# Dense tokens first through the mixer, dense key rankings beside the gathered tokens' mixer, u tiles and rows spread anew, and another order of the gate matrix

## The chip, the cores and the metric

The kernel runs on one core of a Trainium2 chip. The metric is the device time of one execution in microseconds. Times of a kernel are given as the median of several runs; the profile is of one more execution.

## The reference, cut to what matters

One layer of a hybrid decoder over 512 prompt tokens and 64 sample tokens (8 sequences of 8). The mixer is a sliding-window attention with sinks beside a convolution module; after it comes PEER, a retrieval of single-neuron experts.

```python
def layer(x):
    xn = rms_norm(x, norm1_g)
    q, k, v, glu = _project(xn, w_in, q_norm_g, k_norm_g)
    a = attention(q, k, v, sinks)                     # window 128; samples also see 128 cached keys
    c = _conv_module(pad(glu), w, b, ln_g, ln_b, pw)  # depthwise, width 31, then layer norm, silu, @ pw
    h = x + concat(rms_norm(a), rms_norm(c)) @ w_out
    return h + _peer(rms_norm(h, norm2_g), wq, keys, u, v)

def _peer(xt, wq, keys, u, v):                        # u, v: 16384 experts x 1024
    q = (xt @ wq).reshape(T, 8, 2, 128)
    s = einsum('thpd,hpnd->thpn', q, keys)            # 8 heads x 2 halves x 128 keys
    ts, ti = top_k(s, 16)
    best_s, pos = top_k(all 256 sums of the two halves' scores, 16)
    idx, gate = the experts of pos, softmax(best_s)
    hu = einsum('chkd,cd->chk', u[idx], xt)
    return einsum('chk,chkd->cd', gelu(hu) * gate, v[idx])
```

## The kernel before

The 576 tokens stand in five tiles of `TILES`. Tiles 0 to 2 (tokens 0 to 383, `DT` = 384) are the dense tokens: for them u and v are multiplied whole, 128 tiles of 128 experts each, and a gate matrix picks the experts. Tiles 3 and 4 (`TA`, `TB`, 128 + 64 tokens, `GT` = 192) are the gathered tokens: GpSimd fetches, for each of 384 rows, the u or v vectors of 128 token-expert pairs with an indirect DMA into a ring of `SLOTS` = 8, and VectorE multiplies and sums them (`row`).

All order is written out by hand, each engine running its own list, tied by semaphores. The stages, with their starts in the profile:

- The mixer for all 576 tokens. Its matmuls take the columns in two halves of 288 (`HALF`, `two`). After the projections come eight attention units `u` (block of 128 queries, key-value head): scores `S` (L590), softmax on VectorE (`softmax_max`, `softmax_div`) with the exponentials on ScalarE, transposes `PT` (L601), values `O` (L612). Between these TensorE computes the GLU's gemms or the taps of the last conv channel block, and VectorE the taps of the other three (`conv_quarter`, L1457), in slots given by `CONV_AT`. Then the sample attention `SS`, `PTS`, `OS`, and the tail: means, variances, pointwise and output gemms (L524), the second norm (L1224).
- The gathered tokens' queries and key scores (`wqa`, `sca`, 16 blocks) with the rankings `key_ranks("a", ..)`: five VectorE instructions for each tile and block (L1245 to L1249). From 410 us.
- `picks(TA)` and `picks(TB)`: the best 16 of the sums, and the experts' numbers. Between their parts stand calls of `low(n)` (L1234), the low half of u tile `n`, which TensorE's `dense_u(n)` waits for (24 matmuls, L711). 17 u tiles (`U_TOP`), and the first two dense query blocks. From about 485 us.
- 16 blocks of dense queries, scores and rankings (`wqb`, `scb`, `key_ranks("b", ..)`, three tiles), each with one u tile and three rows (`ROWS_RANK`). From about 583 us.
- `picks` of the three dense tiles, 12 u tiles and 6 rows each. From about 731 us.
- The gate stage: 64 batches (`NBAT`) of 6 tokens: VectorE writes two tables of ones (`onehots`, L1397), ScalarE puts the gates in (L997), TensorE multiplies them (L761), ScalarE copies the product to `Gs` (L1013), and SP stores four batches at a time. 54 u tiles (`u_at`) and 152 rows (`batch_rows`) are spread over the batches. From about 891 us.
- The v stage: for each of 128 tiles `mt` = gelu x gates (L1420), its high and low parts `ah` (ScalarE) and `al` (L1428), `low` of the v tile (L1234), 18 matmuls (L783), and the rest of the rows (`v_rows`, 166). The gates come in groups of 16 expert rows (`JG`), two groups in `Gl`; the 16 loads of a group are issued one per tile during the group before (`load_gates`). From about 1284 us.

PSUM is handed out by `psum_plan` as four pairs of banks; `take`, `ready`, `R` and `F` tie each use to the one before it. SP's list holds the weight loads (`load_block`, ring of four), the u and v tiles (`load_raw`, three), and the stores.

Of the kernel before, what the change touches and what calls it, by code (L numbers as in the profile page):

```python
# [43 lines left out]
SLOTS = 8  # L44
# [16 lines left out]
U_RANK = U_TOP + NM  # L61
U_GATE = U_RANK + 12 * DTI
# [8 lines left out]
ROWS_RANK = 3  # L71
ROWS_PICK = 6
B_ROW0 = ROWS_RANK * NM + ROWS_PICK * DTI
V_ROW0 = B_ROW0 + 152

# [13 lines left out]
EXP_AFTER = {6: TA, 14: TB, 39: 0, 51: 1, 63: 2}  # L89
KEYS_AFTER = {8: TB, 33: 0, 45: 1, 57: 2}  # L90
GELU_AFTER = {29: 0, 56: 1}
# [20 lines left out]
BLOCKS += ["woa0", "woa1", "woa2", "pw0", "pw1"] + [f"woa{_m}" for _m in range(3, DC)] + [f"wob{_m}" for _m in range(DC)]  # L112
NMIX = len(BLOCKS)
ROW_WO = BLOCKS.index("woa0") + 2
BLOCKS += [f"wqa{_m}" for _m in range(NM)] + [f"wqb{_m}" for _m in range(NM)]


def block_row(n):

    name = BLOCKS[n]  # L120
    if name[:2] == "wo":
        return ROW_WO + int(name[3:])
    if name[:2] == "pw":
        return ROW_WO - 2 + int(name[2:])
    return n if n < NMIX else ROW_WO + DC + (n - NMIX) % NM


def block_use(n):
# [6 lines left out]
    return {"pw0": "pw1", "pw1": "pw3"}.get(name, name)  # L135


CONV_AT = [0, 0, 0, 1, 2, 3, 4, 5, 6, 7, 8, 9, 10, 11, 12, 12, 12]
# [6 lines left out]
def psum_plan():  # L145

    plan = [("ms1", 3), ("K", 0), ("Q0", 1), ("Kn", 3), ("Q1", 2), ("Q0n", 3), ("Q2", 0), ("Q1n", 3), ("Q3", 1),
            ("Q2n", 3), ("V", 2), ("Q3n", 3)]
    for u in range(8):
        plan += [(f"S{u}", 2)] + ([(f"glu{2 * u}", 0)] if u < CC else []) + [(f"PT{u}", 3)]  # L150
        plan += ([(f"glu{2 * u + 1}", 1)] if u < CC else []) + [(f"O{u}", 2)]
    plan += [("taps", 0)]
    plan += [("SS", 2), ("PTS", 3), ("OS", 2), ("msA", 3), ("mean", 0), ("woa0", 2), ("var", 1)]
    plan += [("woa1", 3), ("woa2", 2), ("pw0", 0), ("pw1", 1), ("pw2", 3), ("pw3", 0), ("woa3", 2), ("msC", 1)]
    plan += [("woa4", 3), ("woa5", 0), ("woa6", 2), ("woa7", 3)]
    plan += [(f"wob{m}", m % 3) for m in range(DC)]
    plan += [("ms2", 3)]
    for m in range(NM):
        plan += [(f"wqa{m}", m % 2)]
        if m:  # L160
            plan += [(f"sca{m - 1}", 2 + (m - 1) % 2)]
# [8 lines left out]
def hymba_peer(nc, xT_d, wblk_d, cols_d, maskp_d, masks_d, ident_d, ckT_d, cv_d, state_d, keysT_d, u_d, v_d, uT_d,  # L170
# [7 lines left out]
    with ExitStack() as ctx:  # L178
# [188 lines left out]
        def _(sp):  # L367
# [72 lines left out]
            for m in range(NM):  # L440
                if m < RAWS:
                    load_raw(m)
# [1090 lines left out]
```

## Time and profile before

| | |
|---|---|
| median of 3 runs | 1841.26 us (1835.47 to 1842.4) |
| the profiled execution | 1849.16 us, span 1847.3 us |
| TensorE busy | 1669.8 us, 90% |
| VectorE busy | 1432.0 us, 78% |
| ScalarE busy | 770.1 us, 42% |
| GpSimd busy | 550.0 us, 30% |
| DMA | 477.45 MB, mean 258 GB/s |
| granted TensorE clock, mean | 0.953 |

The span is from the first to the last instruction of the profiled execution. Busy time is the time in which an engine has at least one instruction under way; matmuls are pipelined, so the distance between the starts of two of them is shorter than their durations, and the same holds, less so, for VectorE. `PE` is TensorE's matmuls, `PEld` its weight loads, `DVE` VectorE, `ACT` ScalarE, `POOL` GpSimd, `SP` the engine that issues most DMAs.

### The profile page before, as it was taken

Reading aid. Unit: us, or ns where it says so; the run is one execution under the profiler, and the core shown is the slowest. Engines: PE = TensorE matmul, PEld = TensorE weight load, DVE = VectorE, ACT = ScalarE, POOL = GpSimd, SP = SyncE. Lnnn points to the kernel's source line nnn. Section 1 sums busy time; section 2 is a strip of 40 time slices with the busy share of each in tenths; the row PEclk is TensorE's granted clock in tenths of the full one; section 3 lists DMA queues with packets and bytes.
Section 4 is the critical chain, followed back from the end, with each engine's and each line's share of the span. In section 5 each row is a group of like instructions: output and inputs, shape, how many; then the busy total and the mean of one; then the engine's idle time right before and its main releaser. Section 6 shows DMA issues by size and latency. Waiting matters only on the chain.

```text
span 1847.3 us, 23140 instructions
## 1 busy us (share of the span) xinstructions
PE 1669.8 (90%) x8361; PEld 1447.9 (78%) x8361; DVE 1432.0 (78%) x2657; ACT 770.1 (42%) x1274; POOL 550.0 (30%) x395
## 2 busy tenths in 40 slices
PE   7887678989699998999889898998999999999997
PEld 5766446769697877999889898998877877877876
DVE  3466854338778999787899999994888888988976
ACT  3222112212242222444789888883333333333332
POOL 0000000000011333111477676661344443443430
PEclk9998887999899999999999999999999999999999
DMA  6110500125275877777699999999999999999985
GB/s 192 46 46 1 66 1 13 50 68 194 89 247 184 277 281 228 248 235 234 216 415 407 406 413 402 381 403 389 363 371 371 375 362 381 387 358 365 379 306 184
DMA packets 164360, 477.45 MB, mean 258 GB/s; under 512 B 28063, under 2 KB 61535, under 8 KB 162071
## 3 DMA queue, kind: packets, MB, share of 16 engines
q1 hardware_dynamic: 108951, 274.63, 42.7%
q0 software_dynamic: 55296, 201.35, 28.7%
q8 instruction: 67, 1.10, 0.2%
q14 instruction: 46, 0.38, 0.1%
HBM read 420.93 MB, written 54.42 MB: 257 GB/s over the span
## 4 chain that ended last, share of the span: by engine, by line
PE 55%; DVE 33%; issue 5%; ACT 3%; DMA 2%; SPq 0%; DVEq 0%; ACTq 0%
PE ps L783 24%; PE ps L711 14%; PE ps L524 9%; DVE ring L1349 8%; DVE lo L1234 4%; DVE acc L1353 2%; DVE gA L1397 2%; DVE gB L1397 2%; DVE cacc L1457 2%; DVE tsi L1246 2%; PE ps L536 2%; DVE tsi L1249 2%; DVE sm L1247 2%; DVE tsv L1248 1%; DMA gelu_matrix<-gest 1%
## 5 line engine op out<-in xcount | busy, mean ns | idle before, releaser
L1057 POOL DMA_INDIRECT ring<-in_u,idx x192 | 281.6, 1467 | 889.1 <-DVE ijg L1329 528.4
L1234 DVE TENSOR_TENSOR lo<-raw,hi 128x1024 fp32r<-128x1024 f32 x256 | 312.9, 1222 | 138.3 <-ACT hi L916 132.2
L916 ACT ACTIVATE hi<-raw 128x1024 fp32r<-128x1024 f32 x256 | 270.4, 1056 | 330.7 <-PE ps L783 323.9
L711 PE MATMUL ps<-xh,hi 128*128 128x384 f32 x1024 | 356.1, 348 | 28.2 <-DVE lo L1234 20.2
L1057 POOL DMA_INDIRECT ring<-in_v,idx x192 | 266.9, 1390 | 369.4 <-DVE acc L1353 351.2
L711 PE MATMUL ps<-xl,hi 128*128 128x384 f32 x1024 | 348.0, 340 | 0.0
L711 PE MATMUL ps<-xh,lo 128*128 128x384 f32 x1024 | 347.5, 339 | 0.0
L783 PE MATMUL ps<-hi,ah 128*128 128x512 f32 x768 | 241.6, 396 | 23.1 <-DVE al L1428 23.0
L1353 DVE SCALAR_TENSOR_TENSOR acc<-ring,hu,acc 128x1024 f32<-128x1024 f32 x192 | 245.6, 1279 | 1.6
L783 PE MATMUL ps<-lo,ah 128*128 128x512 f32 x768 | 240.0, 394 | 0.0
L783 PE MATMUL ps<-hi,al 128*128 128x512 f32 x768 | 239.6, 394 | 0.0
L1349 DVE CUSTOM_DVE_ANT_0 ring<-ring,xtok 128x1024 f32<-128x1024 f32 x192 | 226.2, 1216 | 0.3 <-DVE hu L1349 0.3
L711 PEld LDWEIGHTS ps<-xh,hi 128*128 128x128 f32 x1024 | 197.7, 193 | 31.0 <-DVE lo L1234 22.9
L711 PEld LDWEIGHTS ps<-xl,hi 128*128 128x128 f32 x1024 | 197.2, 193 | 0.0
L711 PEld LDWEIGHTS ps<-xh,lo 128*128 128x128 f32 x1024 | 196.6, 192 | 0.0
L783 PEld LDWEIGHTS ps<-hi,ah 128*128 128x128 f32 x768 | 146.2, 191 | 56.6 <-DVE lo L1234 20.9
L783 PEld LDWEIGHTS ps<-lo,ah 128*128 128x128 f32 x768 | 146.6, 191 | 31.1
L783 PEld LDWEIGHTS ps<-hi,al 128*128 128x128 f32 x768 | 146.3, 190 | 31.0
L942 ACT ACTIVATE gest<-ps 128x384 f32<-128x384 f32 x128 | 63.4, 495 | 251.8 <-PE ps L711 210.7
L681 PE MATMUL ps<-xn,wring 128*128 128x192 f32 (+1 forms) x512 | 133.6, 416 | 5.6 <-DVE xn L1224 5.6
L1013 ACT ACTIVATE Gs<-ps 128x768 f32<-128x768 f32 x64 | 132.3, 2067 | 0.5 <-PE ps L761 0.5
L761 PE MATMUL ps<-gB,gA 128*128 128x128 f32 x768 | 103.3, 288 | 32.0 <-issue 18.4
(176 smaller groups left out, 1971.8 us busy)
## 6 DMA issues: line engine op xcount, KB each, us to landing
raw<-in_uT SPq DMA_DIRECT2D x128, 512.0 KB
raw<-in_v SPq DMA_DIRECT2D x128, 512.0 KB
wring<-in_wblk SPq DMA_DIRECT2D x48, 512.0 KB
gelu_matrix<-gest SPq DMA_DIRECT2D x64, 384.0 KB
gate_matrix<-Gs SPq DMA_DIRECT2D x16, 1536.0 KB
Gl<-gate_matrix SPq DMA_DIRECT2D x128, 192.0 KB
gel<-gelu_matrix SPq DMA_DIRECT2D x128, 192.0 KB
wring<-in_wblk SPq DMA_DIRECT2D x16, 256.0 KB
```

Source lines behind the costliest of these rows:

```text
L524: mm = nc.tensor.matmul(out[:, a * 512:a * 512 + HALF], w, rhs[:, k, a * HALF:(a + 1) * HALF], start=(k == 0), stop=(k == kc - 1))
L681: mm = nc.tensor.matmul(out[:, 0:w], wring[:, n % RING, k * P:(k + 1) * P], xn[:, k, t0:t0 + w], start=(k == 0), stop=(k == DC - 1))
L711: mm = nc.tensor.matmul(out, a[:, n % 2, w], b[:, c, :], start=(c == 0 and k == 0), stop=(c == DC - 1 and k == 2))
L761: mm = nc.tensor.matmul(ps[b % ABUF][:, c:c + NKEY], A[:, b % ABUF, t, :], B[:, b % ABUF, t, :], start=True, stop=True)
L783: mm = nc.tensor.matmul(ps[t][:, h * 512:(h + 1) * 512], a[:, n % 2, w], b[:, n % 2, h * 512:(h + 1) * 512], start=False, stop=(n == NKEY ...
L916: nc.scalar.activation(hi[:, s % 2, :], raw[:, s % RAWS, :], ACT.Copy).then_inc(s_hi, 1)
L1013: nc.scalar.activation(dst, src, ACT.Copy).then_inc(s_gev, 1)
L1057: pool.indirect_dma_start(ring[:, r % SLOTS, :], None, table, bass.IndirectOffsetOnAxis(idx[:, t, c:c + 1], 0)).then_inc(g_in[r % SLOTS], 16)
L1234: nc.vector.tensor_tensor(lo[:, s % 2, :], raw[:, s % RAWS, :], hi[:, s % 2, :].bitcast(F32), ALU.subtract).then_inc(s_lo, 1)
L1349: nc.vector.tensor_tensor_reduce(got, got, xtok[:, t, :], 1.0, 0.0, ALU.mult, ALU.add, hu[:, t, c:c + 1]).then_inc(g_used, 1)
L1353: nc.vector.scalar_tensor_tensor(out=acc[:, t, :], in0=got, scalar=hu[:, t, c:c + 1], in1=acc[:, t, :], op0=ALU.mult, op1=ALU.add).then_in ...
L1397: nc.vector.tensor_tensor(dst[:, b % ABUF], iota.unsqueeze(1).broadcast_to([P, BATCH, NKEY]), kT3[:, half, tok:tok + BATCH].unsqueeze(2).b ...
```

## The change

- The dense tokens pass the mixer first: attention units 0 to 5, the conv module and the output gemms for tokens 0 to 383 (`conv_a`, `group_gemm`, 384 columns). The units 6 and 7, the sample attention and the mixer of the 192 gathered tokens (`conv_b`, `mgb`, `ATb`, `caccb`) come after, with the 16 blocks of dense queries, scores and rankings between their parts on every engine (`block_b`, `ranks_b`).
- Then the gathered tokens' queries and rankings, as before. The two stages between the picks of the gathered and the dense tokens go: the picks of the dense tokens take 15 u tiles and 15 rows each. 61 u tiles and 130 rows are left for the gate stage, and 209 rows for the v stage.
- PSUM is planned by single banks (`held`, `after`, `region`).
- `Gs` and `Gl` hold, within a group of 16 expert rows, the token outside and the expert row inside. ScalarE's copy of a batch now writes runs of 16 elements, where it wrote single elements 24 apart; `mt` reads one element in 16 of `Gl`, where it read runs of 24. The transfers keep their sizes and runs.
- The ring has 7 slots; the gelu over the rows of the second gathered tile moves into the v stage. SP's list follows, with the first three u tiles fetched ahead of weight block `wo4`.

The diff, cut to its core:

```diff
-SLOTS = 8
+SLOTS = 7
-U_RANK = U_TOP + NM
-U_GATE = U_RANK + 12 * DTI
+U_PICK = 15
+U_GATE = U_TOP + U_PICK * DTI
-ROWS_RANK = 3
-ROWS_PICK = 6
-B_ROW0 = ROWS_RANK * NM + ROWS_PICK * DTI
-V_ROW0 = B_ROW0 + 152
+ROWS_PICK = 15
+B_ROW0 = ROWS_PICK * DTI
+V_ROW0 = B_ROW0 + 130
-GELU_AFTER = {29: 0, 56: 1}
+GELU_AFTER = {44: 0}
+GELU_IN_V = {13: 1}
-CONV_AT = [0, 0, 0, 1, 2, 3, 4, 5, 6, 7, 8, 9, 10, 11, 12, 12, 12]
+CONV_AT = [0, 0, 0, 2, 4, 6, 8, 10, 12, 12, 12, 12, 12]
...
-            Gs = gb("Gs", [P, 2, NKEY, TBLK])
-        Gl = sb("Gl", [P, 2, NBLK, JG, TBLK])
+            Gs = gb("Gs", [P, 2, NG, TBLK, JG])
+        Gl = sb("Gl", [P, 2, NBLK, TBLK, JG])
...
@@ sync: load_gates, and the loads ahead of the picks
+                             gm_d[b].rearrange("p j t -> p (j t)")[:, g * JG * TBLK:(g + 1) * JG * TBLK]).then_inc(
+                if BLOCKS[n] == "wo4":
+                    sp.wait_ge(s_o2, 16 * 15)
+                    for r in range(RAWS):
+                        load_raw(r)
...
@@ tensor: after units 0 to 5 and the dense tokens' mixer
+            def block_b(m):
+                queries(f"wqb{m}", 0, DT)
+                if m:
+                    scores("b", m - 1, range(DTI))
+            block_b(0)
+            block_b(1)
+            unit_transposes(6)
+            unit_scores(7)
+            block_b(2)
+            unit_values(6)
+            block_b(3)
+            unit_transposes(7)
+            sample_scores()
+            block_b(4)
+            unit_values(7)
+            pe.wait_ge(s_conv_b, CC)
+            group_means("meanb", lambda k: caccb[:, k, :], CC)
+            block_b(5)
+            sample_transposes()
+            block_b(6)
+            group_means("varb", conv_b, CC, s_sqc, base=CC)
+            sample_values()
+            block_b(7)
+            group_means("msAb", lambda k: mgb[:, k, :], CC, s_sqa, base=CC)
+            for m in range(CC):
+                group_gemm(f"pwb{m}", lambda k: caccb[:, k, :], CC, cut=(m % 2) * CC, last=(m % 2 == 1), made=s_sw, base=CC)
+            block_b(8)
+            group_means("msCb", conv_b, CC, s_sqcr, base=CC)
+            block_b(9)
+            for m in range(DC):
+                group_gemm(f"wo{m}", lambda k: mgb[:, k, :], DC, made=None if m else s_mg, base=DC)
+                if m >= 2:
+                    square_mean("ms2b", m - 2, DC, DT, GT)
+                if m == 3:
+                    block_b(10)
+            square_mean("ms2b", DC - 2, DC, DT, GT)
+            block_b(11)
+            square_mean("ms2b", DC - 1, DC, DT, GT)
+            for m in range(12, NM):
+                block_b(m)
...
-            for m in range(NM):
-                if m + 2 < NM:
-                    queries(f"wqb{m + 2}", 0, DT)
-                if m + 1 < NM:
-                    scores("b", m + 1, range(DTI))
-                dense_u(U_TOP + m)
-            for n in range(U_RANK, U_GATE):
+            for n in range(U_TOP, U_GATE):
                 dense_u(n)
...
@@ scalar: the copy of a gate batch
-                dst = Gs[:, i % 2, :, o:o + BATCH].rearrange("p j (a t) -> p a t j", a=2)
-                src = ps[b % ABUF][:, :].rearrange("p (a c) -> p a c", a=2)[:, :, 0:3 * NKEY].rearrange(
-                    "p a (t j) -> p a t j", t=3)
+                dst = Gs[:, i % 2, :, o:o + BATCH, :].rearrange("p g t j -> p t g j")
+                src = ps[b % ABUF][:, 0:BATCH * NKEY].rearrange("p (t g j) -> p t g j", t=BATCH, g=NG)
...
@@ vector: the order after the dense tokens' second norm
+            unit_max(6)
+            conv_b(22)
+            conv_b(23)
+            unit_div(6)
+            for c in range(DC):
+                x_low(c)
+            ranks_b(0)
+            unit_max(7)
+            ranks_b(1)
+            unit_div(7)
+            unit_out(6)
+            ranks_b(2)
...
+            unit_out(7)
+            centred("meanb", lambda c: caccb[:, c, :], CC)
+            ranks_b(3, 4, 5)
+            rstd("varb", rsb[:, 1, :])
+            normed(lambda c: caccb[:, c, :], rsb[:, 1, :], CC)
...
+            ranks_b(6)
+            rstd("msAb", rsb[:, 0, :])
+            merged(lambda c: mgb[:, c, :], lambda c: ATb[:, c, :], "ga", rsb[:, 0, :])
+            ranks_b(7)
+            rstd("msCb", rsb[:, 1, :])
...
+            ranks_b(8)
+            for m in range(4):
+                h_added("wo", m, DC, DT, GT)
+            ranks_b(9)
+            for m in range(4, DC):
+                h_added("wo", m, DC, DT, GT)
+            ranks_b(10)
+            rstd("ms2b", rsb[:, 0, :])
+            for c in range(DC):
+                second_norm(c, DT, GT, rsb[:, 0, :])
+            ranks_b(*range(11, NM))
...
-            for m in range(NM):
-                key_ranks("b", m, range(DTI))
-                low(U_TOP + m + 1)
-                for r in range(ROWS_RANK * m, ROWS_RANK * (m + 1)):
-                    row(r)
             for t in range(DTI):
-                r0 = ROWS_RANK * NM + ROWS_PICK * t
-                picks(t, t, range(U_RANK + 12 * t + 1, U_RANK + 12 * t + 13), range(r0, r0 + ROWS_PICK))
+                u0 = U_TOP + U_PICK * t + 1
+                picks(t, range(u0, u0 + U_PICK), range(ROWS_PICK * t, ROWS_PICK * (t + 1)))
...
-                                        Gl[:, g % 2, :, n % JG, :], ALU.mult).then_inc(s_mu, 1)
+                                        Gl[:, g % 2, :, :, n % JG], ALU.mult).then_inc(s_mu, 1)
```

## Rows read from the trace of the kernel before

**Rows 1.** Busy time by stage; stage, length, busy of PE, PEld, DVE, ACT, POOL, clock, DMA, GB/s.
```profile
86.00:274.00 188.00, 142.62 (x604) 102.98 (x602) 127.74 (x270) 36.71 (x92) 0.00 (x0) 0.90 0.17 28
...
274.00:297.00 23.00, 14.82 (x136) 12.00 (x136) 4.30 (x11) 3.14 (x11) 0.00 (x0) 0.61 0.00 1
297.00:410.00 113.00, 104.16 (x417) 80.45 (x417) 40.17 (x40) 25.20 (x35) 0.00 (x0) 0.97 0.17 54
410.00:485.00 75.00, 64.78 (x356) 58.44 (x357) 63.70 (x273) 15.98 (x58) 0.00 (x0) 0.89 0.46 148
485.00:583.00 98.00, 88.79 (x461) 81.70 (x460) 68.34 (x232) 42.79 (x50) 10.59 (x10) 0.95 0.52 168
583.00:731.00 148.00, 141.77 (x667) 113.56 (x666) 138.64 (x456) 36.10 (x59) 50.92 (x44) 1.00 0.78 272
731.00:891.00 160.00, 155.18 (x884) 153.75 (x885) 124.50 (x341) 72.47 (x88) 26.59 (x21) 0.98 0.75 236
891.00:1248.00 357.00, 323.68 (x2045) 321.02 (x2044) 347.63 (x460) 310.48 (x556) 242.09 (x150) 0.96 0.98 386
...
1284.00:1847.00 563.00, 534.40 (x2304) 438.77 (x2303) 471.22 (x550) 188.88 (x256) 213.65 (x157) 0.97 0.94 350
```
**Rows 2.** Timeline of TensorE: start us, duration us, engine, line, operation, count; second part near 419 us.
```profile
641.39 0.34 PE L711 MATMUL ps<-xl,hi 128*128 128x384 f32 x1
...
645.38 5.32 PE L681 MATMUL ps<-xn,wring 128*128 128x384 f32 x16
650.54 0.83 PE L691 MATMUL ps<-keysT,q2T 128*128 128x128 f32 x6
651.12 0.42 PE L711 MATMUL ps<-xh,hi 128*128 128x384 f32 x1
...
418.95 2.87 PE L681 MATMUL ps<-xn,wring 128*128 128x192 f32 x16
```
**Rows 3.** Timeline of VectorE, one block's two rankings; then the taps in the groups by line.
```profile
452.89 0.29 DVE L1245 MAX8 tsv<-sm 128x8 f32<-128x128 f32 x1
...
456.64 0.30 DVE L1245 MAX8 tsv<-sm 128x8 f32<-128x128 f32 x1
...
L1457 DVE SCALAR_TENSOR_TENSOR cacc<-gpad,cols_sb,cacc 128x512 f32<-128x512 f32 x90 | 67.6, 751 | 2.9
L1457 DVE SCALAR_TENSOR_TENSOR cacc<-spad,cols_sb,cacc 128x64 f32<-128x64 f32 x90 | 25.1, 279 | 0.0
```
**Rows 4.** Timeline of VectorE in the gate stage: a row, then two one-hot tables.
```profile
1002.11 1.21 DVE L1349 CUSTOM_DVE_ANT_0 ring<-ring,xtok 128x1024 f32<-128x1024 f32 x1
...
1003.26 0.94 DVE L1397 TENSOR_TENSOR gA<-cols_sb,kT 128x768 f32<-128x768 f32 x1
1004.13 0.94 DVE L1397 TENSOR_TENSOR gB<-cols_sb,kT 128x768 f32<-128x768 f32 x1
```
**Rows 5.** Timeline of VectorE at a group change of the v stage; then TensorE's waits there.
```profile
1350.01 0.56 DVE L1420 TENSOR_TENSOR mt<-gel,Gl 128x384 f32<-128x384 f32 x1 [3.45 <-issue]
1350.48 1.28 DVE L1353 SCALAR_TENSOR_TENSOR acc<-ring,hu,acc 128x1024 f32<-128x1024 f32 x1
1351.68 1.22 DVE L1234 TENSOR_TENSOR lo<-raw,hi 128x1024 fp32r<-128x1024 f32 x1
1352.82 0.55 DVE L1428 TENSOR_TENSOR al<-mt,ah 128x384 fp32r<-128x384 f32 x1
...
PE ps L783 <- DVE al L1428: 23.0, 8, 4.9
```
**Rows 6.** GB/s in 40 equal slices: the v stage, then the gate stage.
```profile
GB/s 304 358 391 391 341 364 400 400 398 309 378 335 404 399 309 371 396 399 388 362 356 402 397 389 320 376 369 400 396 292 375 353 400 400 267 286 342 274 76 149
...
GB/s 36 185 271 413 419 423 409 413 411 417 425 405 407 384 404 384 408 413 420 412 422 410 411 408 413 397 407 385 403 417 379 385 385 342 409 419 414 406 366 406
```
**Rows 7.** ScalarE's groups by line and shape in the gate stage: busy us, mean ns.
```profile
L1013 ACT ACTIVATE Gs<-ps 128x768 f32<-128x768 f32 x63 | 130.2, 2067 | 0.5 <-PE ps L761 0.5
...
L916 ACT ACTIVATE hi<-raw 128x1024 fp32r<-128x1024 f32 x52 | 54.6, 1051 | 3.3 <-DMA raw<-in_uT 3.3
```

More of the change, by code:

```diff
@@ L145, in psum_plan @@
 def psum_plan():
[L147 to L153, printed above, removed]
@@ L537, in means, with group_means @@
                                               src(k)[:, a * HALF:(a + 1) * HALF], start=(k == 0), stop=(k == n - 1))
+                mm.then_inc(ready, 1)
+            def group_means(name, src, n, made=None, base=0):
+                out, ready = take(name)
+                for k in range(n):
+                    if made is not None:
+                        pe.wait_ge(made, base + k + 1)
+                    rhs = src(k)
+                    mm = nc.tensor.matmul(out[:, 0:rhs.shape[1]], on512[:, :], rhs, start=(k == 0), stop=(k == n - 1))
                 mm.then_inc(ready, 1)
@@ new lines, in _, with square_mean @@
+            group_gemm("woa0", attn_a, CC, made=s_mg)
+            group_means("msC", conv_a, CC, s_sqcr)
+            for m in range(1, DC):
+                group_gemm(f"woa{m}", attn_a, CC)
+            group_gemm("wob0", conv_a, CC, made=s_mg, base=CC)
+            group_gemm("wob1", conv_a, CC)
+            def square_mean(name, m, base, t0, w):
+                if m == 0:
+                    take(name)
+                out, ready = region(name), R[use[name][0]]
+                pe.wait_ge(s_sqh, base + m + 1)
+                mm = nc.tensor.matmul(out[:, 0:w], on1024[:, :], xn[:, m, t0:t0 + w], start=(m == 0), stop=(m == DC - 1))
+                if m == DC - 1:
+                    mm.then_inc(ready, 1)
@@ L713, in dense_u, with sample_scores @@
                 mm.then_inc(s_hud, 1)
+            def sample_scores():
+                out, ready = take("SS")
+                for b in range(NDB):
+                    for g in range(NKV):
+                        grp, slot = b // 2, (b % 2) * 2 + g
+                        rows = slice(g * HD, (g + 1) * HD)
+                        o = out[slot * 32:slot * 32 + 32, (grp // 2) * 512 + (grp % 2) * 192:]
+                        q = qS[rows, b * 32:(b + 1) * 32]
+                        nc.tensor.matmul(o[:, 0:WIN], q, ckT[rows, b, :], start=True, stop=True)
+                        mm = nc.tensor.matmul(o[:, WIN:WIN + NS], q, kT[rows, SEQ:T], start=True, stop=True)
+                mm.then_inc(ready, 1)
@@ new lines, in merged @@
+            def merged(dst, src, gain, r):
+                for c in range(CC):
+                    nc.vector.scalar_tensor_tensor(out=dst(c), in0=src(c), scalar=col(gain, c), in1=r,
+                                                   op0=ALU.mult, op1=ALU.mult).then_inc(s_mg, 1)
+            def attn_added(m):
+                p = ready(f"woa{m}")
+                nc.vector.tensor_tensor(hT[:, m, 0:DT], hT[:, m, 0:DT], p[:, 0:DT],
+                                        ALU.add).then_inc(F[use[f"woa{m}"][0]], 1)
@@ L1250, in key_ranks, with picks @@
                 dve.sem_inc(s_l1, 1)
-            def picks(t, slot, lows, rows=()):
+            def picks(t, lows, rows=()):
                 n = RANKED.index(t)
@@ L1258, in picks @@
                 rows = list(rows)
+                share = len(lows), len(rows)
                 def pause():
```

850 lines of the change are left out of this document (490 added, 360 removed).

## The prediction

> **What bounds the kernel now.** I read the busy time by stage first [rows 1]; its columns show which engine fills each stretch. Up to 485 us no engine is full. In the attention units (86 to 274 us) TensorE works 142.6 of 188 us and VectorE 127.7: they take turns. In the mixer's tail (297 to 410) TensorE works 104 of 113 us while VectorE works 40. In the ranking of the gathered tokens' keys (410 to 485) VectorE works 63.7 and TensorE 64.8 of 75 us. From 583 to 891 TensorE is the bound (142 of 148 us, 155 of 160). In the gate stage (891 to 1248) it is VectorE: 348 of 357 us, with TensorE at 324. In the dense v stage (1284 on) it is TensorE again, and there VectorE is 84% busy. Then I read the rate of each kind of step from the timelines [rows 2 to 5], and last the traffic: the DMA queues move about 400 GB/s in most slices of the v stage, at most 404, and 405 to 425 in the gate stage [rows 6]. I read both as lids, close to what the stages ask for.
>
> **The profiled run and the median.** The sum is made against the profiled execution: span 1847.3 us, 1849.2 with what lies around it. The median of the shown runs is 1841.3, so what I get is multiplied by 0.9957.
>
> **Units of cost.** One u tile is 24 matmuls; 23 steps from 641.39 to 645.38 us give 4.17 us. A dense query block takes 5.16 us and its scores 0.58; a block for the 192 gathered tokens 2.87 [rows 2]. Ranking one block's keys takes VectorE 3.75 us for the two gathered tiles [rows 3], so some 5.6 for the three dense ones. A tap of the convolution costs 0.75 + 0.28 us less overlap, 0.98, for 512 and 64 columns [rows 3]; by the slope between the two shapes the 384 columns now done alone cost 0.65 and the gathered 128 + 64 cost 0.58. A u-kind row is 1.15 us and a one-hot table 0.87 [rows 4]; in the v stage mt is 0.47, a v row 1.20, low 1.14, al about 0.47 [rows 5].
>
> **Units and the dense tokens' mixer.** Columns are split 384 + 192 instead of 288 + 288, so TensorE's work is the same. The units 1 to 3 now take 16 taps of 0.65 us (10.4) in each slot where 8 of 0.98 stood (7.8). These lie on the path, since TensorE waits there for the probabilities; I take 9 us more, and unit 4 starts at 192 instead of 183. Only two more units follow, with all the taps: 46 instead of 91 us. The sample attention (23 us [rows 1]) and the units 6 and 7 move behind. The tail needs two thirds of its 104 us, 70, plus a chain of roots, reciprocals and norms of about 13: 83 us. The dense query blocks start at 321 us, where the first query block of before starts at 410.
>
> **Gathered mixer beside the dense key rankings.** TensorE gets 16 x 5.74 = 92 us of query blocks and about 60 of mixer: a third of the tail (35), two units (11), sample attention (14). VectorE gets 16 x 5.6 = 90 us of rankings and about 45 of softmax, norms and additions. Each queue is in order and each block's ranking needs the block before it, so the two don't add up to a perfect overlap: walking both queues, VectorE waits some 6 us each at rankings 6, 7, 9 and 10, and finishes ranking 10 and the second norm at 463 us. SP's weight loads follow in the same order, four deep, one per 5.7 us, and the first three u tiles are fetched behind block wo3, long before they are used. After 463 VectorE alone is late: 5 x 5.6 + 16 x 3.75 + two lows = 90 us. The picks of the gathered tokens begin at 553, against 485 before.
>
> **Picks.** The stretch 485 to 583 loses two query blocks and one score block (10.9 us): 87. The stretch 583 to 731 goes: its 16 query blocks are done, and its 16 u tiles are spread. The dense picks take 45 u tiles instead of 36, and 45 rows instead of 18: 45 x 4.17 = 188 us of TensorE and, at the 160 of before for 36, a little over, 200. VectorE has 160 there. The gate stage begins at 553 + 87 + 200 = 840 us instead of 891: 51 us gained, of which 29 are seven tiles moved on.
>
> **Gate stage.** VectorE: 64 x 1.74 + 61 lows x 1.14 + 130 rows x 1.15 = 331 us (before, with 54 lows, 126 such rows and 26 v rows, 349 of 357). TensorE: 61 x 4.17 = 254 plus the gate matmuls, 324 - 54 x 4.17 = 99 at most, less where fewer idle spells lower the clock: 341 to 353. ScalarE's Gs copy is 2.07 us for 768 elements written one by one at a distance of 96 bytes, while 1024 elements in a row take 1.05 [rows 7]; in runs of 64 bytes I expect 0.9 to 1.2, and even at 2.07 it stays just under TensorE. I take 351; the stage ends at 1191, the unchanged tail behind it (36 us) at 1227.
>
> **v stage: where part of it is given back.** 209 rows instead of 166 fall here, 43 more. VectorE: 128 x 2.08 + 17 x 1.15 + 192 x 1.20 = 516 us, before 465, and about 3 us at each of seven group changes, where mt waits for the gates' transfer: 23 us of TensorE's idle time stand there [rows 5]. The first to the last v matmul takes 553 us. The traffic: 128 x (512 + 192 + 192 KB) + 209 x 512 KB = 227 MB, less 9 MB fetched before the stage; at 403 GB/s 541 us, before 485. VectorE 537, TensorE 553 and the queues 541 now lie within 3%. The gate stage, in that position, ran 2.4% over its fullest engine. I take 569 plus 10 for the end: 579 instead of 563.
>
> **Edits at nothing.** The ring of gathered rows has seven slots instead of eight. In the v stage a row is due every 2.7 us, so seven slots still give 19 us from issue to use; if a gather took longer, each row would wait for it. The gelu over the second tile's rows moves from the gate stage into tile 13 of the v stage, on ScalarE, which is busy 189 of 563 us there [rows 1], well ahead of its first use at row 320. The copy of the gathered queries (qB) stands behind the last norm, while TensorE waits for nothing of it until unit 6.
>
> **mt's strided read.** mt now reads Gl one element every 64 bytes. No row of before shows such a read on VectorE. From below its cost is nothing: runs of 24 elements cost as much as a plain tile, 0.55 us in both L1420 and L1428 [rows 5]; a gain has no source. From above it is the price of the strided write on ScalarE, 2.69 ns an element all in, 1.03 us for 384, so 0.48 more, 61 us for 128 [rows 7]. I take nothing, since the read is on VectorE itself and the run-broken read next to it costs nothing, and keep the other end.
>
> The write row is [rows 7]. The Trainium skill, page SBUF — State Buffer, section Door 1: The DMA port swizzle, says that each access that crosses to a new 16-byte line pays a penalty; this speaks against the change. The trace agrees for ScalarE's write, 2.07 us; for VectorE's read no run here shows it. By that rule the sum would be the second case below; without it, the first.
>
> **The sum and the rivals.**
> First case, 50%: 553 + 87 + 200 + 351 + 36 + 579 = 1806 us of span, 1808 with what lies around, times 0.9957: 1800. Its own range is 1782 to 1820.
> Second, the strided read costs as the strided write does, 27%: VectorE becomes the bound of the v stage, 516 + 61 + 21 = 598, with waits 604, plus 10: span 1841 at this end, 1829 at a price of 0.38 us an instruction. Time 1823. For it: the factor of the write; against it: another engine and direction.
> Third, the other side, 7%: the read costs over 0.6 us more in each mt. From mt = 1.13 us on the v stage eats the whole gain: 1227 + 516 + 31 + 128 x 0.58 = 1848. At 1.5 us the time is 1227 + 547 + 122 = 1896 of span, 1890. Against it: it is over the highest price per element in the trace.
> Fourth, the v stage takes the extra rows in VectorE's spare time and the queues give more than 403 GB/s, 10%: v stage 563, gate stage 347, span 1786: 1780. The gate stage's 425 GB/s speaks for it, the flat slices against it.
> Fifth, the gathered mixer and the rankings don't interleave, 6%: if each in-order queue stands still while the other does its mixer part, half of the 60 us of mixer comes on top: 1806 + 27, time 1827. For it: TensorE and VectorE take turns so in 86 to 274 us.
>
> **Numbers.** The likeliest is 1800. The range 1772 to 1834 holds the first, the fourth, the fifth and most of the second; the third is left out. About 0.5% (9 us) is what a measurement can tell from no change: faster means under 1832. First and fourth wholly, three quarters of the second and half of the fifth: 0.83. Within 0.5%: 0.09. Slower: 0.08.
>
> **What would show it.** The dense query blocks should start at 321 and the picks of the gathered tokens at 553 us; VectorE should have no wait over 7 us between. The gate stage should be 345 to 355 us long and bound by TensorE; Gs near 1 us. mt decides between the first three cases: 0.55, about 1.0, or over 1.13 us. In the v stage look for rows that wait for their gathers and for GB/s over 403. The forecast is wrong if the picks start after 575, or if the v stage exceeds 600.

## The result, and the profile after

| | before | after |
|---|---|---|
| median | 1845.51 us (20 runs) | 1856.54 us (20 runs) |
| ratio | | 1.0046, 95% interval 1.0026 to 1.0066 |
| profiled span | 1847.3 us | 1862.6 us |
| TensorE, VectorE, ScalarE, GpSimd busy | 1670, 1432, 770, 550 us | 1685, 1488, 707, 705 us |
| granted TensorE clock, mean | 0.953 | 0.951 |

The forecast was 1800 us in a range of 1772 to 1834. The changed kernel is slower than the kernel before by about half a per cent, so sign and range are both wrong. Everything up to the v stage came as forecast; the v stage took 638 us instead of 569, in the profiled execution. That execution took 1864.5 us, 8 over the median (three slow ones of the 20, the longest 3344.5 us, are left out of the ratio), so the stage is up to that much shorter in others.

Busy time by stage of the kernel after, which answers to [rows 1]: stage, length, busy of PE, PEld, DVE, ACT, POOL, clock, DMA, GB/s.

```profile
86.00:191.00 105.00, 82.84 (x339) 63.38 (x340) 76.11 (x137) 22.19 (x51) 0.00 (x0) 0.91 0.07 21
191.00:320.00 129.00, 116.27 (x420) 69.41 (x418) 87.02 (x234) 28.16 (x57) 0.00 (x0) 0.96 0.34 71
320.00:460.00 140.00, 136.59 (x686) 101.38 (x687) 95.33 (x355) 41.62 (x100) 0.00 (x0) 0.95 0.30 98
460.00:552.00 92.00, 81.32 (x427) 69.57 (x426) 81.36 (x384) 16.28 (x57) 0.00 (x0) 0.95 0.31 98
552.00:637.00 85.00, 73.91 (x410) 72.86 (x408) 60.89 (x209) 42.48 (x48) 7.30 (x7) 0.93 0.53 172
637.00:833.00 196.00, 189.34 (x1081) 187.10 (x1081) 161.41 (x387) 86.69 (x110) 58.14 (x45) 0.99 0.88 291
834.00:1180.00 346.00, 341.60 (x2203) 340.99 (x2203) 327.11 (x444) 239.39 (x561) 196.25 (x128) 0.98 0.99 382
1181.00:1214.00 33.00, 30.38 (x192) 30.09 (x192) 10.38 (x13) 9.72 (x14) 3.86 (x3) 1.00 1.03 399
1214.00:1852.00 638.00, 562.86 (x2304) 449.22 (x2303) 549.71 (x607) 190.76 (x254) 437.38 (x201) 0.93 0.93 343
```

The gate stage is 5 us shorter than before (346.9 against 352.2, from its first to its last matmul) and starts 62 us earlier. In the last row no engine is full: TensorE works 563 of 638 us, VectorE 550, and the queues move 343 GB/s, less than before [rows 1]. The granted clock is 0.93 there and was 0.97 before; in e10 below, where the waits of mt and of the rows are gone, it is 0.99. GpSimd works 437 us for 201 gathers, where it worked 214 for 157. So I looked for who waits for whom there. The waits of the kernel after in the v stage (us in total, times, longest us):

```profile
POOL ring L1249 <- DVE acc L1613: 134.0, 96, 9.1
PEld ps L913 <- DVE lo L1466: 88.1, 33, 8.2
PE ps L913 <- DVE al L1738: 77.7, 34, 7.8
ACT hi L1030 <- DMA raw<-in_v: 53.3, 16, 4.7
DVE acc L1613 <- DMA ring<-in_v,idx: 34.0, 7, 7.4
DVE mt L1730 <- issue: 32.7, 7, 7.7
```

TensorE's wait for `al` was 23.0 us in 8 pieces before [rows 5]; now it is 77.7 in 34. Three things delay VectorE itself: the group changes (mt, 7 times), late v tiles (through `hi`), and rows that wait for their gathers. The last two are new: in the v stage of the kernel before, neither `hi` nor a row stands among the waits for a transfer. The timelines of GpSimd and VectorE at one such wait:

```profile
1388.61 2.15 POOL L1249 DMA_INDIRECT ring<-in_v,idx  x1 [0.64 <-DVE acc L1613]
1391.41 17.92 POOL L1249 DMA_INDIRECT ring<-in_v,idx  x1 [0.65 <-DVE acc L1613]
1409.64 0.94 POOL L1249 DMA_INDIRECT ring<-in_v,idx  x1 [0.31 <-issue]
...
1406.46 1.27 DVE L1613 SCALAR_TENSOR_TENSOR acc<-ring,hu,acc 128x1024 f32<-128x1024 f32 x1
1407.66 0.84 DVE L1730 TENSOR_TENSOR mt<-gel,Gl 128x384 f32<-128x384 f32 x1
1414.83 1.28 DVE L1613 SCALAR_TENSOR_TENSOR acc<-ring,hu,acc 128x1024 f32<-128x1024 f32 x1 [6.33 <-DMA ring<-in_v,idx]
```

One instruction that writes out a gather lasts 17.92 us, where the ones next to it last 0.94 to 2.15. VectorE works without a gap meanwhile (five tiles), uses up the ring, and then stands still for 6.3 us. 21 of the 201 gathers last over 3 us, 169 us together; before, the longest lasted 2.75 us.

The two shapes that the new order of the gate matrix changes, in the groups by line and shape of the kernel after: VectorE in the v stage, then ScalarE in the gate stage, which answers to [rows 7].

```profile
L1730 DVE TENSOR_TENSOR mt<-gel,Gl 128x384 f32<-128x384 f32 x127 | 105.5, 830 | 32.7 <-issue 32.7
L1738 DVE TENSOR_TENSOR al<-mt,ah 128x384 fp32r<-128x384 f32 x127 | 70.4, 554 | 0.0
...
L1203 ACT ACTIVATE Gs<-ps 128x768 f32<-128x768 f32 x63 | 50.0, 794 | 1.8 <-PE ps L891 1.8
```

The strided read takes 0.83 us, 0.28 more than `al` of the same size. The copy in runs of 64 bytes takes 0.79 instead of 2.07 us.

### The profile page after: what moved, and what is told of

It reads as the page before. It is cut to its first block, busy times and chain, and to the rows that moved or that the text cites. A ratio compares the mean times of both kernels' runs of the same rounds, so it can differ in the third digit from the quotient of the medians.

```text
span 1862.6 us, 23354 instructions
## 1 busy us (share of the span) xinstructions
PE 1685.0 (90%) x8361; PEld 1439.8 (77%) x8361; DVE 1487.5 (80%) x2788; ACT 707.1 (38%) x1310; POOL 705.2 (38%) x395
## 4 chain that ended last, share of the span: by engine, by line
PE 53%; DVE 22%; DMA 11%; issue 7%; ACT 4%; POOL 3%; DVEq 0%; SPq 0%; ACTq 0%
PE ps L763 24%; DMA ring<-in_v,idx 7%; PE ps L913 6%; PE ps L543 5%; PE ps L891 4%; DVE acc L1613 4%; PE ps L559 4%; POOL ring L1249 3%; PE ps L733 3%; DMA raw<-in_v 2%; DVE lo L1466 2%; DVE al L1738 2%; DVE cacc L1321 2%; ACT hi L1030 1%; PE ps L624 1%
## 5 line engine op out<-in xcount | busy, mean ns | idle before, releaser
L1249 POOL DMA_INDIRECT ring<-in_v,idx x192 | 424.9, 2213 | 167.9 <-DVE acc L1613 134.0
L913 PE MATMUL ps<-hi,ah 128*128 128x512 f32 x768 | 253.3, 412 | 77.8 <-DVE al L1738 77.7
L913 PE MATMUL ps<-lo,ah 128*128 128x512 f32 x768 | 247.8, 405 | 0.0
L913 PE MATMUL ps<-hi,al 128*128 128x512 f32 x768 | 245.1, 401 | 0.0
L913 PEld LDWEIGHTS ps<-lo,ah 128*128 128x128 f32 x768 | 151.2, 197 | 33.7
L913 PEld LDWEIGHTS ps<-hi,al 128*128 128x128 f32 x768 | 150.5, 196 | 33.5
L733 PE MATMUL ps<-xn,wring 128*128 128x384 f32 (+1 forms) x512 | 136.3, 421 | 6.2 <-DVE xn L1455 4.1
L1730 DVE TENSOR_TENSOR mt<-gel,Gl 128x384 f32<-128x384 f32 x128 | 106.3, 830 | 33.1 <-issue 32.7
L733 PEld LDWEIGHTS ps<-xn,wring 128*128 128x128 f32 x512 | 91.1, 194 | 43.3 <-issue 11.2
```

The costliest lines, as they stand in the source:

```text
L733: mm = nc.tensor.matmul(out[:, 0:w], wring[:, n % RING, k * P:(k + 1) * P], xn[:, k, t0:t0 + w], start=(k == 0), stop=(k == DC - 1))
L913: mm = nc.tensor.matmul(ps[t][:, h * 512:(h + 1) * 512], a[:, n % 2, w], b[:, n % 2, h * 512:(h + 1) * 512], start=False, stop=(n == NKEY ...
L1249: pool.indirect_dma_start(ring[:, r % SLOTS, :], None, table, bass.IndirectOffsetOnAxis(idx[:, t, c:c + 1], 0)).then_inc(g_in[r % SLOTS], 16)
L1730: nc.vector.tensor_tensor(mt[:, n % 2, :].rearrange("p (a b) -> p a b", a=NBLK), gel[:, n % EG, :].rearrange("p (a b) -> p a b", a=NBLK), ...
```

## The experiments

Each time is a median, each ratio is to the kernel before on the same chip. The two lengths are from the first to the last matmul of the stage in the profiled run. That is one execution: most are within 2 us of their median, but those of after, before, e3 and e9 are 8, 4, 2 and 4 us over it, and those of e2, e6 and e8 5, 11 and 4 under. "Gathers" is how many of GpSimd's gather instructions in the v stage last over 3 us, and the longest.

| kernel | us | ratio (95%) | gate | v | gathers |
|---|---|---|---|---|---|
| before | 1845.5 | | 352.2 | 552.6 | 0, 2.8 |
| after | 1856.5 | 1.0046 (1.0026 to 1.0066) | 346.9 | 637.8 | 21, 17.9 |
| e1_old_layout | 1842.9 | 0.998 (0.9955 to 1.0004) | 360.5 | 601.9 | 0, 2.8 |
| e2_before_new_layout | 1852.3 | 1.0034 (1.0005 to 1.0063) | 347.5 | 553.7 | 11, 7.6 |
| e3_before_7_slots | 1843.2 | 0.9998 (0.9982 to 1.0013) | 350.1 | 552.4 | 0, 2.7 |
| e4_before_209_rows | 1885.7 | 1.02 (1.0149 to 1.0252) | 341.7 | 603.8 | 0, 3.0 |
| e5_after_166_rows | 1831.3 | 0.9917 (0.9888 to 0.9946) | 388.0 | 557.9 | 7, 4.1 |
| e6_half_v_tiles | 1834.7 | 0.9957 (0.9929 to 0.9985) | 346.8 | 596.8 | 33, 17.9 |
| e7_short_low | 1822.5 | 0.9889 (0.9872 to 0.9905) | 344.1 | 599.0 | 3, 4.6 |
| e8_old_layout_166_rows | 1813.4 | 0.9865 (0.9819 to 0.991) | 381.3 | 544.7 | 0, 2.8 |
| e9_after_early_gates | 1831.8 | 0.9941 (0.9913 to 0.997) | 347.0 | 608.7 | 24, 17.9 |
| e10_old_layout_early_gates | 1803.7 | 0.9773 (0.9725 to 0.982) | 358.6 | 564.5 | 0, 2.8 |
| e11_old_166_early_gates | 1793.5 | 0.9715 (0.9669 to 0.9762) | 385.6 | 524.7 | 0, 2.8 |
| e12_old_166_early_20_in_picks | 1779.9 | 0.9645 (0.9599 to 0.9691) | 368.1 | 525.2 | 0, 2.8 |
| e14_padded_mt | 1809.8 | 0.9831 (0.9789 to 0.9874) | 360.4 | 568.1 | 0, 2.8 |
| e15_old_184_early_20_in_picks | 1782.6 | 0.9675 (0.9634 to 0.9716) | 360.7 | 537.0 | 0, 2.8 |

One thing the column of gathers shows at once: the six kernels with the strided read (after, e2, e5, e6, e7, e9) all have gathers over 3 us, and none of the ten others has one.

### The order of the gate matrix, or the number of rows

My first theory, R, put the v stage's loss on the strided read; its rival, N, on the 43 more rows. Two kernels undo one of the two in the changed kernel, two put one of them into the kernel before.

e1_old_layout:

```diff
-            Gs = gb("Gs", [P, 2, NG, TBLK, JG])
-        Gl = sb("Gl", [P, 2, NBLK, TBLK, JG])
+            Gs = gb("Gs", [P, 2, NKEY, TBLK])
+        Gl = sb("Gl", [P, 2, NBLK, JG, TBLK])
...
-                                        Gl[:, g % 2, :, :, n % JG], ALU.mult).then_inc(s_mu, 1)
+                                        Gl[:, g % 2, :, n % JG, :], ALU.mult).then_inc(s_mu, 1)
```

> The changed kernel with the gate matrix in the old order again (Gs, Gl, ScalarE's copy, mt's read), nothing else. In the changed kernel the first to the last v matmul takes 638 us, before 553. Theory R (mt's strided read): mt falls from 0.83 to 0.55 us, which frees 36 us of VectorE in a v stage where it has no gap, so that GpSimd's gathers are no longer held up; the v stage falls to 575 to 595 us and the ratio to before is 0.965 to 0.98. Theory N (the 43 more rows alone overload the gathers): mt falls as well, but the gathers stay late, the v stage stays over 615 us and the ratio is over 0.99. Either way Gs goes back to 2.07 us and the gate stage stays within 5 us of 347, since ScalarE's 328 us stay under TensorE's 343.

The v stage falls by 35.9 us to 601.9, between the two. (The two ratios, less the gate stage's share, give some 26 us instead of 36.) The gate stage grows by 13.6 us, which I had not expected: with Gs at 2.07 us ScalarE works 315 of 360 us there, and TensorE waits for it eight times, 10.5 us in all. Each of these waits ends with `gA`, the gates that ScalarE puts into a batch's table, and each time ScalarE had just stood 2.8 to 4.1 us for the store of a gelu tile (`gest`). The kernel after has one such wait of TensorE, 0.4 us.

e4_before_209_rows:

```diff
-V_ROW0 = B_ROW0 + 152
+V_ROW0 = B_ROW0 + 109
-GELU_AFTER = {29: 0, 56: 1}
+GELU_AFTER = {38: 0}
+GELU_IN_V = {13: 1}
```

> The kernel before with 43 rows moved from the gate stage to the v stage (109 and 209 instead of 152 and 166), old order of the gate matrix. Theory N: v stage 620 us or more, as in the changed kernel (638), gathers of over 3 us on GpSimd, gate stage some 20 us shorter; ratio over 1.02. Theory R: VectorE has 516 of 553 us, the v stage grows to 565 to 590 and the gate stage shrinks to about 335: ratio 0.995 to 1.01.

The kernel before with the rows of the changed one: v stage 603.8, 51 us more for 43 rows, without any strided read and, against theory N, without any long gather; the length lies between what the two theories said. The gate stage gives back only 10.5.

e2_before_new_layout (the same edit as e1, the other way round, in the kernel before) and e5_after_166_rows (43 rows moved back to the gate stage):

```diff
-V_ROW0 = B_ROW0 + 130
+V_ROW0 = B_ROW0 + 173
-GELU_AFTER = {44: 0}
-GELU_IN_V = {13: 1}
+GELU_AFTER = {36: 0, 60: 1}
+GELU_IN_V = {}
```

> The kernel before with the new order of the gate matrix only. Theory R: mt costs 0.83 us, VectorE gets 36 us more in a v stage where 92 us were idle; if full occupancy is what hurts, the v stage grows by 10 to 30 us and gather instructions over 3 us appear on GpSimd; ratio 1.00 to 1.015, as the gate stage, bound by VectorE, gains little from the faster Gs. Theory N: the extra VectorE time lies in gaps, v stage within 5 us of 553, ratio 0.995 to 1.003, no gather instruction over 3 us.

> The changed kernel, new order kept, with 43 rows moved back from the v stage to the gate stage (173 and 166). Gate stage: VectorE 331 + 49 = 380 us, so about 385 to 390 instead of 347. Theory N: v stage back to 555 to 565 us, ratio 0.975 to 0.985. Theory R: mt at 0.83 still loads the v stage, 570 to 590 us, ratio 0.985 to 1.0.

With 166 rows the strided read costs little in the v stage: 553.7 against 552.6 in e2. (The ratio of e2, 1.0034, is higher than theory N allowed; its profiled execution, 5 us under the median, doesn't show where the time goes.) But long gathers do appear, 11 of them, as theory R said. In e5 the v stage is back at 557.9, and the gate stage takes the rows at 388 us; the ratio, 0.9917, is higher than theory N said, in the range of R. Against e8 below, which differs from e5 only in the order of the gate matrix, the v stage of e5 is 13.2 us longer. So by the profiles the rows alone cost 51 us, the read alone 1 to 13, both together 85. Both theories hold a part, and the parts don't add: some 20 to 33 us come only with the two together.

### What the rows cost: the last load of a group of gates

In e4 and e1 VectorE is only 86% busy, and the queues move 361 to 363 GB/s on average. GB/s of e1_old_layout in 40 slices of its v stage:

```profile
GB/s 361 390 401 401 323 321 379 401 402 367 319 383 402 401 380 338 375 402 400 371 299 358 402 401 399 295 362 401 400 401 269 376 398 401 401 255 358 360 390 89
```

Between the dips the queues stand at about 400: the lid of [rows 6] holds. There are seven dips, one for each group change. SP issues one of the 16 loads of the next group after each tile, so the sixteenth is asked for when the last mt of the group is done, and the next mt needs it. With free queues that costs 3 to 4 us [rows 5]; with full ones the load stands behind others (median 9.3 us from issue to landing in e1, and mt waits 6.8 us each time), and while VectorE waits little else is asked for. The test issues the loads in the first 12 tiles of a group:

```diff
-                if n // JG + 1 < NG:
-                    load_gates(n // JG + 1, n % JG)
+                if n // JG + 1 < NG and n % JG < 12:
+                    for b in range(n % JG * NBLK // 12, (n % JG + 1) * NBLK // 12):
+                        load_gates(n // JG + 1, b)
```

> The changed kernel with the old order of the gate matrix, 209 rows in the v stage, and the gates' loads early as described. Theory G: 218.7 MB at 402 GB/s are 544 us, TensorE's own 553 less its 25 us of waits at group changes 530: the v stage falls from 602 to 550 to 570 us, at 385 GB/s or more; ratio 0.97 to 0.98. Rival L: 363 GB/s as before, over 590 us, ratio over 0.99.

> The changed kernel, where SP issues the 16 loads of the next group of gates during the first 12 tiles of a group instead of one per tile, so that the last is not asked for right before it is needed. Same bytes. Theory G (the queues give 402 GB/s as I assumed, and the v stage loses what it loses at its seven group changes): the v stage falls from 638 to 590 to 610 us, since mt's waits (33 us) and the queues' idle slices go, while 15 or more gathers still take over 3 us; ratio 0.985 to 0.993. Rival L (the stage's mix of transfers gives about 363 GB/s at best, and the dips only shift): the v stage stays over 625 us.

Theory G holds in both (the ratio of e9, 0.9941, is just outside). Without the strided read the v stage falls from 601.9 to 564.5, with it from 637.8 to 608.7. The dips are gone; GB/s and waits of e10_old_layout_early_gates in the v stage:

```profile
GB/s 372 400 401 400 403 401 398 399 401 395 399 399 398 395 385 397 401 399 400 403 400 400 400 400 396 389 401 400 397 404 403 399 398 401 400 354 391 400 376 93
...
POOL ring L1250 <- DVE acc L1614: 224.6, 182, 5.9
ACT hi L1030 <- DMA raw<-in_v: 193.9, 60, 6.6
...
PE ps L913 <- DVE al L1739: 27.2, 27, 3.7
```

Now the stage is bound by the transfers: 218 MB in 564 us, and `hi` waits 194 us for its tile. mt itself no longer stands among the waiting.

### What the strided read costs

44 us are left between e9 (608.7) and e10 (564.5). mt's own 0.28 us are 36 us of VectorE, which has them to spare in e10 (516 of 564). Either the queues are late and the long gather instructions follow from it (T), or VectorE holds GpSimd up (P).

e6_half_v_tiles:

```diff
-                sp.dma_start(raw[:, s % RAWS, :], src).then_inc(r_in[s % RAWS], 16)
+                w = D if s < NKEY + 3 else D // 2
+                sp.dma_start(raw[:, s % RAWS, 0:w], src[:, 0:w]).then_inc(r_in[s % RAWS], 16)
```

> The changed kernel, where each v tile is loaded only in its left half of the columns (the right half of the result is not that of the reference): 33 MB less traffic in the v stage, with VectorE's and GpSimd's work as it was. Theory T (the transfers are late, and the long gather instructions follow from the backlog): gathers over 3 us go from 21 to under 5, the v stage takes 570 to 595 us, the ratio to before is 0.965 to 0.98. Rival P (VectorE without gaps holds up GpSimd's gather instructions whatever the queues do): at least 15 gathers over 3 us are left, and the v stage takes over 610 us.

With 33 MB less, at 312 GB/s, 33 gathers last over 3 us. So full queues don't cause them. The v stage falls by 41 us all the same, to 596.8, as mt's waits fall from 32.7 to 3.7 us and those of `hi` for its tile from 53.3 to 5.8. P is right on the gathers. On the length neither was, but the size is not sure: this profiled execution is the fastest of ten, 11 us under their median, and that of the changed kernel 8 over its own; by the two ratios the kernel gains 16 us, not 41.

e7_short_low:

```diff
-                nc.vector.tensor_tensor(lo[:, s % 2, :], raw[:, s % RAWS, :], hi[:, s % 2, :].bitcast(F32),
-                                        ALU.subtract).then_inc(s_lo, 1)
+                w = D if s < NKEY + 2 else D // 2
+                nc.vector.tensor_tensor(lo[:, s % 2, 0:w], raw[:, s % RAWS, 0:w], hi[:, s % 2, 0:w].bitcast(F32),
+                                        ALU.subtract).then_inc(s_lo, 1)
```

> The changed kernel, where the low half of each v tile is made for 512 of 1024 columns only (the rest of the low half is stale, so the result is less exact): VectorE has 128 x 0.55 = 70 us less in the v stage, the traffic is as it was. Theory T: the v stage stays over 625 us, and 15 or more gathers take over 3 us. Rival P: with gaps on VectorE no gather, or up to 3, takes over 3 us, and the v stage falls to the 600 us that 209 rows cost with the old order of the gate matrix.

With 484 of 599 us on VectorE three gathers are long, 4.6 us at most, and the v stage takes what e1 takes: P again. Left was whether a VectorE that is busy all the time is enough or the stride is needed. e14_padded_mt gives the kernel of e10 the time without the stride:

```diff
+                nc.vector.tensor_tensor(spare[:, 0:128], gel[:, n % EG, 0:128], gel[:, n % EG, 128:256], ALU.mult)
+                nc.vector.tensor_tensor(spare[:, 128:144], gel[:, n % EG, 0:16], gel[:, n % EG, 128:144], ALU.mult)
```

> The kernel with the old order of the gate matrix, 209 rows in the v stage and early gates (1803.7 us), with two idle two-input multiplications of 128 and 16 contiguous elements ahead of each mt in place of the 0.28 us that the strided read takes more: some 0.3 us more of VectorE per tile, without any strided read. Theory F (VectorE without gaps is what stretches GpSimd's gather instructions): 15 or more of 201 take over 3 us, and the v stage takes 585 to 610 us, as the 609 of the changed kernel with early gates. Rival S (the strided read itself is needed for it): no gather over 3 us, and the v stage takes 565 to 580.

The busy time of the v stage in e14_padded_mt (columns as in [rows 1]), and GpSimd's group there:

```profile
1228.00:1796.00 568.00, 551.31 (x2304) 428.67 (x2303) 550.73 (x859) 189.54 (x254) 344.55 (x201) 1.00 1.01 385
...
L1251 POOL DMA_INDIRECT ring<-in_v,idx x192 | 332.0, 1729 | 190.6 <-DVE acc L1615 178.7 <-DVE hu L1611 6.8 <-issue 5.0
```

And the same group in e9_after_early_gates:

```profile
L1250 POOL DMA_INDIRECT ring<-in_v,idx x192 | 434.3, 2262 | 129.2 <-DVE acc L1614 85.4 <-issue 37.1 <-DVE hu L1610 6.8
```

VectorE works 551 us in e14, as many as in e9 (550), and in a shorter stage: 97% busy, with stretches of up to 90 us without any gap. Yet no gather lasts over 2.83 us, and the v stage takes 568. Rival S holds: by the profiles the time costs 3.6 us and the stride 40.6. (By the ratios it is some 11, with intervals that overlap, and some 34.) That the two added instructions are what helps GpSimd is ruled out by e10: it has only the plain mt, VectorE has stretches of up to 41 us without a gap there, longer than any in the kernel after (33), and no gather lasts over 2.8 us.

What the stride does to GpSimd the trace doesn't say. It shows this: of the 48 long gathers of the kernels after, e9 and e7 each has at least one mt in it, 44 have no gap on VectorE before their end, and each ends 0.80 to 0.83 us after the end of a VectorE instruction, as the 17.92 us one above does after its mt. None of this marks a long gather for certain. Most short ones end in the same way (127 of 180 in the kernel after, 165 of 201 in e14); two of the 33 in e6, of 3.25 us, have no mt in them; and 15 of the 18 in e2 and e5, of 4 to 8 us, have a gap of 0.15 to 0.34 us on VectorE.

### Seven slots, and better kernels

e3_before_7_slots:

```diff
-SLOTS = 8
+SLOTS = 7
```

> The kernel before with a ring of seven rows instead of eight, nothing else. If a slot less costs nothing (my step in the prediction), the time is within 0.3% of before and the v stage within 3 us of 553. Rival: the gathers need the lead. Then the v stage is 560 to 575 us long and the ratio 1.004 to 1.012.

It costs nothing, as forecast. (With seven slots in the changed kernel five tiles' rows are used up within a long gather; whether an eighth would hide part of that was not tried.)

e8_old_layout_166_rows (both undone, the rest of the change kept):

> The changed kernel with the old order of the gate matrix and 166 rows in the v stage as before (43 more in the gate stage). If the v stage's length is set by its rows and the order of the gate matrix alone, it takes 553 us, as before, and the gate stage 390 to 400, because VectorE has 376 us there and ScalarE 315: ratio 0.99 to 0.997. Rival: the rest of the change (PSUM by single banks, seven slots) costs something in the v stage; then that takes over 560 us.

1813.4 us, 29 faster than the kernel before: this is what the new order of the mixer is worth, together with the u tiles and rows spread anew ahead of the v stage. The ratio is better than I expected, since the gate stage takes 381 us instead of 390 to 400, and the v stage 545 instead of 553. The last 8 us I can't explain; half of them may be the profiled execution, the fastest of four.

e11_old_166_early_gates and e12_old_166_early_20_in_picks (ROWS_PICK 20, 15 rows less in the gate stage):

> The changed kernel with the old order of the gate matrix, 166 rows in the v stage and the gates' loads early. Theory G: the v stage falls from 545 us by the 25 us that mt waits at group changes, to 518 to 526; ratio 0.97 to 0.976. Rival L: 195.9 MB at 363 GB/s are 540 us, ratio 0.984 or more.

> As the kernel before it, with 20 rows instead of 15 in the picks of each dense tile: 15 rows less in the gate stage, where VectorE works 375 of 381 us, and 15 more where TensorE is the bound (189 of 196 us) and VectorE works 161. I expect the gate stage at 364 to 370 us and the picks at 196 to 200: 8 to 16 us less than the kernel before it. Rival: the rows delay the steps of the picks on which TensorE's transposes and the gates wait, and the picks grow by what the gate stage gives (17 us).

Busy time of the picks, the gate stage and the v stage in e12:

```profile
637.00:838.00 201.00, 190.53 (x1082) 187.15 (x1082) 180.06 (x418) 87.95 (x114) 84.62 (x60) 0.99 0.92 324
838.00:1206.00 368.00, 347.71 (x2209) 341.76 (x2209) 359.53 (x475) 314.71 (x561) 253.36 (x156) 0.99 1.00 397
1241.00:1766.00 525.00, 524.83 (x2302) 433.91 (x2303) 468.75 (x548) 186.14 (x253) 215.72 (x158) 0.99 0.99 374
```

Both came as expected: 20 us by the early gates, 14 more by the rows, where the gate stage gave 17 and the picks took 4. In the v stage TensorE now has no idle time. 1779.9 us is 3.5% under the kernel before and the best of the study.

e15_old_184_early_20_in_picks (18 rows from the gate stage to the v stage):

> The best so far (1779.9 us) with 18 rows moved from the gate stage, where VectorE works 359.5 of 368 us, into the v stage, where TensorE works 524.8 of 525 and the queues give 374 of 402 GB/s: 184 rows there. The gate stage should be 354 to 360 us (VectorE 340, TensorE 346), the v stage 525 to 532 (205 MB at 402 GB/s are 511 us): 4 to 14 us less than 1779.9. Rival: near the lid each late transfer costs TensorE, the v stage grows by over 10 us, and nothing is gained.

The rival was right: the gate stage gives 7 us, the v stage takes 12 (`hi` waits 151 us for its tiles, 9 in e12), at 383 GB/s. Nothing is gained; the intervals of the two ratios overlap.

## Why the prediction was wrong

**The mixer, the rankings and the picks: right.** Unit 4 starts at 191 us (192 forecast), the dense query blocks at 320 (321), the picks of the gathered tokens at 552 (553); they take 85 us (87), and the dense picks 196 (200). The gate stage starts at 834 instead of 840. One sign missed: VectorE had a wait of 8.7 us in between, at 396 us, where I had said 7 at most. The fifth case, no interleaving, did not occur: TensorE works 137 of the 140 us from 320 on.

**Gate stage: right in length, wrong in a reason.** 347 us (351), TensorE 342. But "even at 2.07 it stays just under TensorE" was no reason to expect the same time: e1 shows that the slow copy costs 13.6 us. Being under the bound in sum was not enough, since ScalarE, once held up by a store, has no time left to catch up, and TensorE waits for its gates. With 43 rows more in the stage VectorE is the bound (376 us), and there the fast copy gains nothing: 388 us in e5, 381 in e8; why it is longer stays open.

**The lid of the queues: right, but the stage can't use it to its end.** I took 403 GB/s; e10 stands between 395 and 404 in 33 of 40 slices. Its last slice moves 93, and the mean is 387, so the 218 MB for which I took 541 us took 564.5.

**The group changes: the step that failed first.** I took "about 3 us at each of seven group changes" from a stage whose queues had time to spare, and added 2.4% for three full resources. But the wait is for a load that stands in the same queues, so it grows as they fill: mt waits 26.6 us in the kernel before, 47.1 in e4, and each wait empties the queues that set the stage's length. The term of 21 us (seven times 3) measured 37.4: e1 takes 601.9 us, e10 without these waits 564.5. That e10 comes near the forecast of 569 says nothing for it: the 569 held the 21 us of waits, so the rest of the stage stood at 548, and that measured 564.5. The overlap of three resources within 3% of each other was taken 17 us too short as well.

**mt's strided read, "I take nothing": the step that failed second, and the largest.** It costs 0.28 us, inside my bounds (0 to 0.48). By the second case's formula that is 516 + 36 + 21, some 573 us of VectorE, and would hardly have shown; e14 confirms that this much time costs 3.6 us. What no case held is the effect on another engine: GpSimd's gather instructions of up to 18 us, 36 us of the v stage (after against e1), 41 with early gates (e9 against e14), or 26 and 34 by the ratios. VectorE waits 34.0 us for gathered rows in the kernel after, which is about as much. The rule of the Trainium skill cited with this step, page SBUF — State Buffer, section Door 1: The DMA port swizzle, on crossing to a new 16-byte line, gives no size; both measured differences go its way, 2.07 to 0.79 us for the write and 0.55 to 0.83 for the read.

**Seven slots at nothing: right alone (e3).** "If a gather took longer, each row would wait for it" was the sentence that came true, and I put no chance on it. The trace of before has no gather over 2.75 us, so its price could not be read there, but its place could have been named as a rival.

**The slower side.** The third case wanted mt at 1.13 us; mt was 0.83 and the kernel slower all the same. Its accounting saw VectorE's own sum as the only way for the v stage to grow. Against the forecast the v stage was 69 us too long: 16 for the group changes, 17 for the rest of the stage without a strided read, 36 for the strided read. Against the kernel before it grew by 85 us, and there the group changes are the smaller part, as they cost 20 us already with 166 rows (e8 against e11). The 43 rows cost 57 us: 40 apart from the group changes (e11 against e10, which is bound by the transfers) and 17 in longer group changes. The strided read costs 36 more. The 8 us by which e8 is shorter than the kernel before, and which I can't explain, count the other way.

The Trainium skill, page SBUF — State Buffer, section Who interferes with whom, says that a VectorE instruction with two SBUF inputs contends with a GpSimd instruction that reads SBUF. mt, lo, al and acc all have two such inputs. The gather instruction reads its indices there. This case agrees only in part: gather instructions lengthen somewhat as VectorE fills (1361 ns on average before, 1729 in e14), but with the same instructions 97% busy none exceeds 2.83 us, and only with the strided read do they reach 17.9. That section has nothing on a stride.

## What to carry to other kernels

A load that is issued right before its use costs little while the queues have room and much once they are full; ask for it some tiles earlier before you move more traffic into its stage (20 us in e11, 37 in e10, by three lines). Before you trade a strided write on one engine for a strided read on another, look at who else works in the stretch of the read: the 0.28 us that the read itself takes was the smaller part of its price. And when every sum of a stage lies within 3% of the others, take the price of each wait from a stretch that is as full, or forecast wide.

## What was not expected of the hardware

- GpSimd's instruction for a gather of 128 rows, 0.94 us alone, lasted up to 17.9 us (21 of 201 over 3 us) beside a VectorE one of whose instructions reads one fp32 element in each 64 bytes; without that stride, at the same VectorE load, 2.83 us at most. The longest stand where VectorE has no gap; with small gaps they reach 4 to 8 us (e2, e5). How the two are tied stays open.
- The price of a stride differs by engine and direction: 768 elements on ScalarE, written 96 bytes apart, took 2.07 us against 0.79 in runs of 64 bytes; 384 elements on VectorE, read 64 bytes apart as one of two inputs, took 0.83 against 0.55.
- The queues held about 400 GB/s for nearly all of 500 us, with runs of 4 KB and 1.5 KB and from both SP and GpSimd (e10).
